# Rotation of queries and keys: VectorE takes each pair one item later, and ScalarE moves all four quarters

## What is computed

```python
def apply_rope(t, cos, sin):
    t1, t2 = jnp.split(t.astype(jnp.float32), 2, axis=-1)
    ...
    return jnp.concatenate([t1 * c - t2 * s, t2 * c + t1 * s], axis=-1)
...
for l in range(DEPTH):
    ...
    p = h @ w_in[l]
    qkv = p[..., :i0].reshape(B, S, 3, ATT_HEADS, HEAD_DIM)
    q = apply_rope(qkv[:, :, 0], cos, sin)
    k = apply_rope(qkv[:, :, 1], cos, sin)
    y_att = dilated_mixture_attention(q, k, qkv[:, :, 2]).reshape(B, S, ATT_WIDTH)
    y_rwkv = rwkv7_time_mix(p[..., i0:i1], ...)
```

## Time and profile before

| | us |
|---|---|
| median of 3 runs | 2398.1 (2397.48 to 2398.43) |
| the profiled execution | 2395.14 |
| its span in the profile | 2393.3 |
| PE busy | 2311.8 (97%) |
| DVE busy | 1645.6 (69%) |
| ACT busy | 1212.4 (51%) |
| POOL busy | 27.9 (1%) |

### The profile page before, as it was taken

How to read it: one execution, slowest core, us unless ns; L and a number is a source line. 1 busy time by engine, 2 the same in 40 slices (tenths; PEclk the granted TensorE clock), 3 DMA queues, 4 the chain that set the end, 5 groups by cost and what they waited for, 6 DMA issues and landing times.

```text
span 2393.3 us, 42745 instructions
## 1 busy us (share of the span) xinstructions
PE 2311.8 (97%) x18286; PEld 2163.6 (90%) x18286; DVE 1645.6 (69%) x2399; ACT 1212.4 (51%) x1905; POOL 27.9 (1%) x28
## 2 busy tenths in 40 slices
PE   7999998999999999999999999999999999999999
PEld 6888988998888898999999888899899989889998
DVE  7777468997696647676676577766666666767665
ACT  4744334554564445455445447644555445575453
POOL 0000000000001000000000000100000000010000
PEclk8999999999999999999999999999999999999999
DMA  9444445777545334555555533455545554245554
GB/s 366 155 142 142 142 167 192 243 254 255 206 135 175 106 127 148 184 179 176 168 185 184 170 114 106 150 181 185 179 160 181 185 181 136 89 150 177 182 184 132
DMA packets 115293, 411.16 MB, mean 172 GB/s; under 512 B 12784, under 2 KB 15984, under 8 KB 114976
## 3 DMA queue, kind: packets, MB, share of 16 engines
q1 hardware_dynamic: 114816, 408.05, 51.1%
q10 hardware_dynamic: 288, 0.39, 0.0%
HBM read 407.32 MB, written 1.06 MB: 171 GB/s over the span
## 4 chain that ended last, share of the span: by engine, by line
PE 83%; DVE 8%; ACT 6%; issue 1%; DMA 1%; POOL 1%; SPq 0%; ACTq 0%; DVEq 0%; POOLq 0%
PE bank L195 82%; ACT arena L239 3%; DVE lo L202 2%; DVE arena L210 2%; DVE arena L202 2%; ACT hi L239 2%; DVE acc L210 1%; ACT L239 1%; DMA arena<-WA 1%; PE bank L199 1%; POOL arena L202 1%; DVE arena L213 0%; DVE rs_t L216 0%; DVE m L202 0%; DMA raw<-W 0%
## 5 line engine op out<-in xcount | busy, mean ns | idle before, releaser
L195 PE MATMUL bank<-h,hi 128*128 128x256 f32 (+1 forms) x6880 | 1277.5, 287 | 0.0
L239 ACT ACTIVATE hi<-raw 128x1024 fp32r<-128x1024 f32 x664 | 699.0, 1056 | 823.0 <-PE bank L195 784.7
L195 PEld LDWEIGHTS bank<-h,hi 128*128 128x128 f32 x6880 | 1087.4, 194 | 9.4 <-issue 3.4
L195 PE MATMUL bank<-h,lo 128*128 128x256 f32 x3504 | 1019.1, 291 | 16.6 <-DVE h L210 15.2
L202 DVE TENSOR_TENSOR lo<-raw,hi 128x1024 fp32r<-128x1024 f32 x664 | 806.2, 1220 | 145.4 <-ACT hi L239 143.9
L195 PEld LDWEIGHTS bank<-h,lo 128*128 128x128 f32 x3504 | 678.2, 194 | 32.9 <-issue 12.2
L195 PE MATMUL bank<-act,hi 128*128 128x512 f32 x1056 | 371.6, 393 | 0.0
L195 PE MATMUL bank<-act,lo 128*128 128x256 f32 x1056 | 301.0, 285 | 0.0
L195 PE MATMUL bank<-arena 64*64 64x64 f32 (+7 forms) x2994 | 247.4, 262 | 17.3 <-DVE arena L202 10.7
L195 PEld LDWEIGHTS bank<-act,hi 128*128 128x128 f32 x1056 | 198.4, 188 | 45.2
L195 PEld LDWEIGHTS bank<-arena 64*64 64x64 f32 (+3 forms) x2994 | 188.5, 146 | 55.1 <-DVE arena L202 14.1
(11 more groups left out here) (145 smaller groups left out, 1981.8 us busy)
## 6 DMA issues: line engine op xcount, KB each, us to landing
raw<-W SPq DMA_DIRECT2D x664, 512.0 KB, 3.4
ada<-WA SPq DMA_DIRECT2D x80, 512.0 KB, 4.3
arena<-WA SPq DMA_DIRECT2D x16, 512.0 KB, 12.3
arena<-scr SPq DMA_DIRECT2D x2, 1024.0 KB, 9.8
xT<-x SPq DMA_DIRECT2D x1, 1024.0 KB, 7.6
arena<-lora SPq DMA_DIRECT2D x2, 512.0 KB, 9.2
arena<-wsT SPq DMA_DIRECT2D x2, 512.0 KB, 10.1
arena<-lnb SPq DMA_DIRECT2D x2, 512.0 KB, 10.4
```

Of the source, the lines that this page charges most:

```text
L195: return self.done(lambda e: e.matmul(out, l, r, start=start, stop=stop, skip_group_check=True))
L239: return self.done(lambda e: e.activation(out, in_, f, scale=scale, **kw))
```

## The change

On DVE the rotation becomes a function `rope(l, p)` and loses its two copies. It is called for pair p - 1 at the end of item `("qk", l, p)` for p = 1 to 3, and for the last pair at the start of item `("v", l)`, ahead of that item's tiles. ACT moves all four quarters and with the last of them frees the bank and signals `swap`; POOL waits for ACT's signal in place of DVE's.

```diff
+            def rope(l, p):
+
+                o, s = qk[:, p * 512:(p + 1) * 512], sw[:, (p % 2) * 512:(p % 2 + 1) * 512]
+                v.wait_ge(a_main, ("swap", l, p))
+                v.wait_ge(d_cst, "cst")
+                v.tt(two(o), two(o), bc(C("cos"), 1, [128, 2, 256]), MUL).then_inc(v_main, ("cos", l, p))
+                v.wait_ge(v_main, ("cos", l, p))
+                v.wait_ge(g_main, ("sin", l, p))
+                v.tt(o, o, s, ADD).then_inc(v_main, ("qk", l, p))
+
...
                 elif what in ("gmlp v", "v"):
+                    if what == "v":
+                        rope(q[0], 3)
                     f.tiles(32)
...
                 elif what == "qk":
                     l, p = q
                     f.tiles(16)
-                    o, s = qk[:, p * 512:(p + 1) * 512], sw[:, (p % 2) * 512:(p % 2 + 1) * 512]
-                    v.wait_ge(a_main, ("swap", l, p))
-                    v.copy(s[64:96, :], ps(item)[96:128, :]).then_inc(v_main)
-                    v.copy(s[96:128, :], ps(item)[64:96, :]).then_inc(v_main, ("swap", l, p), frees=item)
-                    v.wait_ge(d_cst, "cst")
-                    v.tt(two(o), two(o), bc(C("cos"), 1, [128, 2, 256]), MUL).then_inc(v_main, ("cos", l, p))
-                    v.wait_ge(v_main)
-                    v.wait_ge(g_main, ("sin", l, p))
-                    v.tt(o, o, s, ADD).then_inc(v_main, item)
+                    if p:
+                        rope(l, p - 1)
...
                     a.act(o, ps(item), ACT.Copy).then_inc(a_main)
-                    a.act(s[0:32, :], ps(item)[32:64, :], ACT.Copy).then_inc(a_main)
-                    a.act(s[32:64, :], ps(item)[0:32, :], ACT.Copy).then_inc(a_main, ("swap", l, p))
+                    for r in (0, 32, 64, 96):
+                        a.act(s[r:r + 32, :], ps(item)[r ^ 32:(r ^ 32) + 32, :], ACT.Copy).then_inc(
+                            a_main, *([("swap", l, p)] if r == 96 else []), frees=item if r == 96 else None)
...
-                    g.wait_ge(v_main, ("swap", l, p))
+                    g.wait_ge(a_main, ("swap", l, p))
                     g.tt(two(s), two(s), bc(C("sin"), 1, [128, 2, 256]), MUL).then_inc(g_main, ("sin", l, p))
```

## The result

| | before | after |
|---|---|---|
| median, us (runs of the same comparison) | 2398.07 (2397.48 to 2398.43, 4 runs) | 2384.83 (2382.69 to 2388.48, 4 runs) |
| profiled execution / its span, us | 2395.1 / 2393.3 | 2386.85 / 2385.0 |
| mean granted clock | 0.981 | 0.980 |
| ratio of the medians, 95% interval | | 0.995 [0.9937, 0.9963] |

The change makes the kernel 0.5% faster, 13.2 us. The direction was right, and the steps in the stage came out almost as forecast. The rest came from elsewhere, and most of this part is about where.

The account below looks back on a forecast made before the run. PE, busy 2311.8 of 2393.3 us, was taken as the bound, gaining only where it waits for DVE. 3.82 + 0.2 = 4.0 us a layer, 8.0 in both: 2398.1 - 8.0 = 2390.1 us, range 2387.0 to 2394.2.

Parts of the forecast that it names:

- The bound: PE's four waits for DVE at `merge` in each layer's stage are all the change can remove: 10.2 us in both.
- the three waits: PE's waits at `merge` for pairs 0 to 2 go whole: 3.82 us a layer.
- The fourth wait: PE's wait at the last pair's `merge`: of 1.29 us some 0.2 goes and 1.1 stays.
- ACT: Two more quarters an item start ACT's next split 0.4 us later; nobody waits, so nothing was charged.
- POOL goes first: Rival, chance 0.10: POOL's product holds up DVE's for the last pair; a layer gains 3.4 us, giving 2391.3 us.
- The sum in the stages: Three waits and part of the fourth: 4.0 us a layer, 8.0 us in both.
- Everything after the stage starts from PE's progress and moves forward with it: Behind the stage: no backlog on DVE into which the stage's 8.0 us gain could go.
- one or two stretches more: Rival, chance 0.14: more lower-clock stretches after small matmuls take back 2.4 to 4.8 us, giving 2392.5 to 2394.9 us.
- the better case: Chance 0.04: more gain than forecast, by one lower-clock stretch fewer (2387.7 us) or by the fourth wait gone.
- The prediction's own sign: Forecast would be wrong if the clock in 190 to 260 or 770 to 840 us came out at another level.
- Runs of one kernel differ by 1 us here: Scatter between whole-kernel runs, taken as 1 us when setting the range.

Follow-up runs that it names:

- late_only: Kernel before with each pair's rotation one item later on DVE, but DVE still copying its two quarters; 2387.41 us, ratio 0.9959.
- quarters_only: Kernel before with ACT moving all four quarters, the rotation left at its old place on DVE; 2392.33 us, ratio 0.998.
- mid_layer0: Changed kernel with the last pair's rotation moved to the middle of item v in layer 0 only; 2383.04 us, ratio 0.9949.
- early_cos: Changed kernel with DVE's product by the cosines let go after ACT's first copy, ahead of the quarters; 2386.28 us, ratio 0.9962.
- after_pad6: Changed kernel with 6 repeated matmuls (0.7 us) behind item v of layer 1; 2389.0 us, ratio 0.9961.
- last_mid_v: Changed kernel with the last pair's rotation moved to the middle of item v in both layers; 2389.22 us, ratio 0.9963.
- before_pad12: Kernel before with 12 repeated matmuls (1.4 us) behind item v of layer 1; 2402.8 us, ratio 1.0027.
- after_pad12: Changed kernel with 12 repeated matmuls (1.4 us) behind item v of layer 1; 2391.99 us, ratio 0.9977.
- after_pad18: Changed kernel with 18 repeated matmuls (2.2 us) behind item v of layer 1; 2391.12 us, ratio 0.9975.

## Why the prediction was right in its direction and wrong in its size

**The bound, and the three waits.** Right. PE's waits for DVE were what could be had. The three went whole: late_only's stage is 3.82 and 3.85 us shorter, the forecast's figure.

**The fourth wait.** Right in kind, too small by 0.14 us: forecast 0.2, measured 0.34 in quarters_only and after. The shift that the prediction worked out from ACT's end is there: the last sum starts 7.45 us behind `merge` (169.13 to 176.58), before 7.67 (173.73 to 181.40), 0.22 less. The other 0.12 is between split and mask, where the mask follows the split's start by 1.13 us now (177.19 to 178.32), before by 1.25. It goes with the copies: 1.13 in quarters_only too, 1.25 in late_only. Why it does is open.

**ACT.** Right: nobody waits for its later split. No new wait for ACT's `hi` appears in either stage.

**POOL goes first.** It did not come true. In the last pair DVE's product started first (174.83 against 174.88), and POOL was the one held: 1.60 against 1.09 us. For pairs 0 to 2 the prediction counted 0.5 us of hold-up, and there was none: POOL took 1.09 us and was through before DVE came to the rotation. The prediction looked only for DVE's loss at that port, and had no row for POOL alone without DVE; that 0.5 us already sat in the old wait, where POOL took 1.59 us.

**The sum in the stages.** Forecast 4.0 us a layer, measured 4.12 to 4.20. With 8.3 us in place of 8.0 the forecast would have been 2389.8 us, no nearer to the result in any way that counts.

**The step that failed: "Everything after the stage starts from PE's progress and moves forward with it".** It moves forward, but to places in time at which the chip grants it another clock. The sum put this term at nothing. The rivals knew the mechanism ("the change moves where they fall") but priced it almost only against the change: 0.14 for one or two stretches more, and 0.04 for the better case, which stood for one stretch fewer, 2387.7. It happened on the better side, and came out larger: 5.1 us less of clock lost behind 760 us (6.8 in the third profile), worth 2.9 us of time in the tail. The prediction's own sign of it is there: the granted clock in 770 to 840 us is 0.90 in all four profiles of before and 0.93 in all three of after. In 190 to 260 us it moves between 0.88 and 0.95 in both kernels alike, so that sign says nothing. Nothing in the profile of before says which sign a shift gives. Against before, and without added work, the tail is shorter in the change (-2.9), late_only (-2.9), mid_layer0 (-2.5), quarters_only (-2.2) and early_cos (-2.0), the same in after_pad6, and longer in last_mid_v (+1.7), before_pad12 (+1.8 to its end), after_pad12 (+2.8 to its end) and after_pad18 (+5.4). So both signs deserved a like chance.

**The other step: "Runs of one kernel differ by 1 us here".** This was taken from three runs. 61 runs of the kernel before lie between 2392.64 and 2402.57 us (median 2397.48, mean 2396.9, standard deviation 2.7), 15 runs of the kernel after between 2381.29 and 2389.75 (median 2383.87, mean 2384.5). The profiled execution 3.0 us below the median was the sign of it, and I used it as a fixed offset. With two medians of a handful of runs each, some 2 us of pure scatter belonged into the range on either side; 2387.0 as a lower end had room for neither that nor a second step of clock.

**The account.** The pooled means differ by 12.5 us: 8.3 in the two stages, 2.9 in the tail. The remaining 1.3 us lies ahead of the stages, between them, or in the scatter of means of 61 and 15 runs (0.7 us by their deviations); no profile shows it as a difference of the kernels, and it stays open.

**What stays open.** That the tail's clock hangs on the moment at which its work falls is shown by the padded kernels. Which property of the moment decides is not. The Trainium skill, "TensorE: Matmul & The Clock Gate", section "What's actually happening", says that the watching behind the gate runs freely and does not start anew with a kernel. That would suit the first 700 us, which scatter from run to run. It does not by itself explain a tail that repeats within 0.1 us in four profiles of the kernel before. The traces show how far the repeating goes: the last low stretch ahead of layer 1's stage begins 53.2 to 53.5 us ahead of it in all sixteen profiles, though the stage starts anywhere from 709.0 to 720.4 us. So the lower level already stands at a fixed place relative to the work there, and a shorter stage brings the tail nearer to it. And what counts is not simply how near: quarters_only and early_cos, whose stages differ by 3.3 us, have the same low stretches at the same distances behind the stage (the first at 54.9 us) and lose the same 17.1 us. What brings the level to that fixed place no run here settles.

## What to carry to other kernels

When an engine that sets the pace waits for another at a step of each period, look at what stands in the other's order ahead of the operation that is waited for, and move behind it whatever is not needed until a period later; that alone was worth 3.8 of some 4.2 us a layer, and the copies handed to an idle engine were mostly slack. Put into the range of such a forecast what the clock may do with the shifted work behind it, in both directions and by measured steps, even if no changed instruction is there. And to compare variants that differ by a few microseconds, compare the stage itself and the spans at equal clock, since medians here mix a gain of 1 us with a clock that moves by 5.

## What the runs showed of the hardware

A shift of 0.7 us in the middle of the kernel, by six repeated matmuls, changes the clock lost behind it from 15.4 to 20.5 us. That is one profile of the padded kernel; its four runs lie within 2.1 us. The loss comes in steps of 1.7 us. None of it falls in the stage itself, though PE stands there for up to 1.66 us at a time. Of the seven low stretches behind it in the kernel before, four hit PE at work throughout (the longest, 10.2 us from 820.25, follows 6.39 us of 32 small matmuls from 815.14), and three take in a stand of PE, the first from 963.61 with 4.49 of 6.82 us busy.

POOL's product of 128x512 takes 1.09 us while DVE is idle (early_cos, 173.59), 1.09 us too when DVE masks Y with one of its two inputs in PSUM (after, 155.53), and 1.60 us when DVE's own product of two SBUF inputs has started 0.05 us before it. This agrees with the rule quoted ahead of the result from the Trainium skill, "SBUF — State Buffer", section "Who interferes with whom", in the direction that the prediction had not weighed: the first to start keeps the port, and here the loser was POOL, with DVE then waiting 1.06 us for it.
